# Linear attention beside a projection: decay exponents as differences of one kept sum, and low weight parts made by an adding DMA

## The reference, cut to what matters

```
cum   = cumsum(log_a)                                   # per channel k
att   = einsum('bthk,bshk,btshk->bhts', q, k, exp(cum_t - cum_s))   for s <= t
o     = att @ v + (q * exp(cum)) @ state
state = exp(cum_end) * state + (k * exp(cum_end - cum))^T @ v
```

## Time and profile before

| | |
|---|---|
| median of 3 runs | 1741.18 us (1737.77 to 1741.54) |
| the profiled execution's own time | 1737.67 us |
| its span | 1736.0 us |
| granted TensorE clock over the span | 0.988 |
| first projection in the span | about 44 to 295 us |

### The profile page before, as it was taken

One profiled execution on the slowest core, in us unless ns is written; L12 is line 12 of the kernel. 1 busy time (PEld: TensorE's weight loads), 2 busy tenths in 40 slices (PEclk: granted clock), 3 DMA queues, 4 the chain that ended last, 5 costly groups with the idle time before them and its releaser, 6 DMA issues. The chain is left out here.

```text
span 1736.0 us, 26342 instructions
## 1 busy us (share of the span) xinstructions
PE 1673.0 (96%) x10174; PEld 1416.8 (82%) x10174; DVE 1320.9 (76%) x2484; ACT 852.0 (49%) x1481; POOL 67.4 (4%) x120
## 2 busy tenths in 40 slices
PE   5899999799999999999999998999999999999998
PEld 1688877687888888878888657988898988999997
DVE  2777884786999999969984788599875555765586
ACT  3724345646555542256663665333354567665541
POOL 0940000000000000000000000000000000000000
PEclk7999999999999999999999999999999999999999
DMA  8543431042232236734554335444465554434443
GB/s 301 191 138 121 124 121 48 1 146 84 99 97 98 97 101 213 245 132 158 176 185 136 96 93 171 163 158 148 156 203 177 164 175 148 134 123 134 146 158 110
DMA packets 70325, 246.03 MB, mean 142 GB/s; under 512 B 8031, under 2 KB 9752, under 8 KB 69816
## 3 DMA queue, kind: packets, MB, share of 16 engines
q1 hardware_dynamic: 67736, 240.47, 42.3%
q10 hardware_dynamic: 2080, 2.76, 0.5%
q0 software_dynamic: 384, 1.11, 0.2%
HBM read 242.87 MB, written 1.18 MB: 141 GB/s over the span
## 5 line engine op out<-in xcount | busy, mean ns | idle before, releaser
L506 PE MATMUL banks<-m,weights_high 128*128 128x256 f32 (+1 forms) x4144 | 980.6, 330 | 10.0 <-DVE weights_low L373 7.2
L506 PEld LDWEIGHTS banks<-m,weights_high 128*128 128x128 f32 x4144 | 696.8, 190 | 90.1 <-issue 9.7
L506 PE MATMUL banks<-m,weights_low 128*128 128x256 f32 (+1 forms) x2072 | 676.9, 327 | 0.0
L373 DVE TENSOR_TENSOR weights_low<-weight_ring,weights_high 128x1024 fp32r<-128x1024 f32 x293 | 355.0, 1222 | 190.3 <-ACT weights_high L367 189.3
L506 PEld LDWEIGHTS banks<-m,weights_low 128*128 128x128 f32 x2072 | 392.7, 190 | 34.4
L367 ACT ACTIVATE weights_high<-weight_ring 128x1024 fp32r<-128x1024 f32 x293 | 309.1, 1057 | 223.3 <-DMA weight_ring<-in_weights 130.4
L675 DVE SCALAR_TENSOR_TENSOR m<-m,columns 128x189 f32<-128x189 f32 (+4 forms) x504 | 199.2, 470 | 11.5 <-ACT m L613 11.4
L831 DVE SCALAR_TENSOR_TENSOR m<-weight_ring,m 128x1024 bf16<-128x1024 f32 x160 | 195.8, 1224 | 8.2 <-ACT m L810 2.5
L506 PE MATMUL banks<-m,weight_ring 128*128 128x256 f32 x704 | 152.1, 379 | 0.0
L506 PEld LDWEIGHTS banks<-m,weight_ring 128*128 128x128 f32 x704 | 133.7, 190 | 18.1
L612 ACT ACTIVATE m<-banks,columns 128x512 f32<-128x512 f32 (+1 forms) x76 | 58.4, 768 | 170.4 <-PE banks L506 166.5
(11 more groups left out here) (423 smaller groups left out, 1720.6 us busy)
## 6 DMA issues: line engine op xcount, KB each, us to landing
weight_ring<-in_weights SPq DMA_DIRECT2D x433, 512.0 KB, 3.7
m<-entering SPq DMA_DIRECT2D x28, 256.0 KB, 3.2
x<-in_tokens SPq DMA_DIRECT2D x2, 1024.0 KB, 9.0
m<-in_cmp_w SPq DMA_DIRECT2D x1, 2048.0 KB, 7.4
m<-in_cond SPq DMA_DIRECT2D x2, 512.0 KB, 4.3
m<-entering POOLq DMA_DIRECT2D x4, 256.0 KB, 5.0
out<-x ACTq DMA_DIRECT2D x8, 128.0 KB, 2.0
m<-in_rg_w ACTq DMA_DIRECT2D x1, 512.0 KB, 3.5
```

The costliest lines, as they stand in the source:

```text
L373: dve.tensor_tensor(K.w_lo[:, g % PARTS, :], K.ring[:, PLACE[PRODUCT_BLOCKS[g]] % RING, :], K.w_hi[:, g % PARTS, :].bitcast(F32), ALU.subt ...
L506: mm = pe.matmul(out, lhsT, rhs, start=p.start and i == 0, stop=p.stop and i == len(passes) - 1)
```

## The change

It has two halves.

**Exponents.** The eighth `distances` moves to the front: PE makes the sums over each 128-token block once (`sums`, at the tick of level 1), ACT copies them out of PSUM into a kept tile `sums`, and the seven `distances` of the levels are gone. At level l DVE subtracts, from each element of the kept sum, that of its block's middle (two instructions of 128 x 1024), ACT takes the exponential in four pieces of 128 x 512 with the sign in `scale`, in place, and DVE multiplies as before. The scores of level l are made at the tick of level l+1 (one tick later), and DVE takes them up two ticks behind that, just ahead of the multiplications of level l+1. POOL makes only the masks of the levels (28 `affine_select` in place of 84), and the two strict masks later.

**Low parts.** For the projection's blocks from the ninth on (`BY_DMA`, blocks 8 to 30: 23 of them), DVE no longer subtracts. ACT writes the negated high part into `weights_low` (128 x 1024, behind a wait for its own high part), and POOL issues a DMA that adds the weight block from DRAM to it (`accum_op=ALU.add`, 512 KB each). PE waits for its landing, on one semaphore for each of the four buffers. The ring's place is released by the high part and not by the low part.

```diff
+EVEN_FIRST = 8
+BY_DMA = set(blocks_of("even_in")[EVEN_FIRST:])
@@ high_part
     act.activation(K.w_hi[:, g % PARTS, :], K.ring[:, place % RING, :], ACT.Copy).then_inc(*K.high_done.up())
+    if PRODUCT_BLOCKS[g] in BY_DMA:
+        act.wait_ge(*K.high_done.now())
+        act.activation(K.w_lo[:, g % PARTS, :], K.w_hi[:, g % PARTS, :].bitcast(F32), ACT.Copy,
+                       scale=-1.0).then_inc(*K.minus_done.up())
...
+def low_by_dma(K, pool, g, n):
+    pool.wait_ge(K.minus_done.sem, n)
+    pool.dma_start(K.w_lo[:, g % PARTS, :], K.dram["weights"][PLACE[PRODUCT_BLOCKS[g]]],
+                   accum_op=ALU.add).then_inc(K.low_landed[g % PARTS].sem, 16)
@@ _run_products
+        if PRODUCT_BLOCKS[g] in BY_DMA:
+            K.low_landed[g % PARTS].up(16)
+            K.parts_ready.append(K.low_landed[g % PARTS].now())
+            K.release[PLACE[PRODUCT_BLOCKS[g]]] = K.high_done.sem, g + 1
+            continue
...
-                    low_part(K, dve, n_low)
+                    if PRODUCT_BLOCKS[n_low] not in BY_DMA:
+                        low_part(K, dve, n_low)
...
+            for g, n in landing:
+                beside.half("gpsimd", pool, 2 * sum(d <= g for d in due))
+                low_by_dma(K, pool, g, n)
@@ GlaSteps.tensor_steps
         for l in range(1, GLEVELS + 1):
-            yield self.level(l)
-            pe.wait_ge(*self.taken.at(l))
-            pe.wait_ge(*self.tabled.at(l))
-            pe.wait_ge(*self.la_made.at(1))
-            distances(self.between[:, 2 * l - 2, :], self.between[:, 2 * l - 1, :])
-            yield self.level(l) + 3
+            if l == 1:
+                yield self.level(l)
+                pe.wait_ge(*self.taken.at(l))
+                pe.wait_ge(*self.la_made.at(1))
+                sums(K.tri_f[:], K.tri_b[:])
+            yield self.level(l + 1)
+            pe.wait_ge(*(self.taken.at(l) if l > 1 else self.sums_kept.at(1)))
             pe.wait_ge(*self.made.at(l))
             scores(self.factor[l % 2][:, 0, :, :], self.factor[l % 2][:, 1, :, :])
-        yield self.SUMS
-        pe.wait_ge(*self.taken.at(GLEVELS + 1))
-        distances(K.tri_f[:], K.tri_b[:])
@@ GlaSteps.scalar_steps
-            act.activation(e, self.banks(), ACT.Exp).then_inc(*self.exps.up())
+        act.activation(self.sums, self.banks(), ACT.Copy).then_inc(*self.sums_kept.up())
+        for l in range(1, GLEVELS + 1):
+            yield self.level(l) + 1
+            act.wait_ge(*self.differenced.at(l))
+            for d in range(2):
+                decay = e[:, 2 * d:2 * d + 2, :].rearrange("p a (b w) -> p (a b) w", w=size)
+                for part, sign in ((late, 1.0 - 2.0 * d), (early, 2.0 * d - 1.0)):
+                    ins = act.activation(decay[:, :, part], decay[:, :, part], ACT.Exp, scale=sign)
+            ins.then_inc(*self.exps.up())
@@ GlaSteps.vector_steps
+            yield self.level(l)
+            for d, middle in enumerate((half - 1, half)):
+                decay, total = (a[:, 2 * d:2 * d + 2, :].rearrange("p a (b w) -> p (a b) w", w=size) for a in (e, self.sums))
+                ins = dve.tensor_tensor(decay, total, total[:, :, middle:middle + 1].broadcast_to([P, 2 * T // size, size]),
+                                        ALU.subtract)
+            ins.then_inc(*self.differenced.up())
+            yield self.level(l) + 2
+            if l > 1:
+                take_scores(l - 1)
             dve.wait_ge(*self.exps.at(l))
```

More of the change, by code:

```diff
@@ L192, in __init__ @@
         self.low_done = count("weights_low_done")
+        self.minus_done = count("weights_high_negated")
+        self.low_landed = [count(f"weights_low_landed{i}") for i in range(PARTS)]
+        self.n_landing = 0
         self.used = count("weights_used")
@@ L1384, in feed_forward @@
                                 finish if half else None, Gate(gated_hi[:, j, :], gated_lo[:, j, :]) if half else None)
-                    rounds.append([Item(tile_products(first + (2 * j + half) * KD, KD,
-                                                      lambda k: h[:, k, :] if plain else K.h_parts(n, k), n), None, "act", conv)])
+                    tile = first + (2 * j + half) * KD
+                    whole = tile // TPB in PLAIN
+                    rounds.append([Item(tile_products(tile, KD, lambda k, whole=whole: h[:, k, :] if whole else K.h_parts(n, k), n),
+                                        None, "act", conv)])
             down = residual_items(K, f"down{layer}", KF, lambda k: (gated_hi[:, k, :], gated_lo[:, k, :]), t0,
@@ L1501, in __init__ @@
         self.la, self.att, self.cend = K.take(TT, 2 * 256), K.take(16, P), K.take(4, TT)
-        self.table = K.take(3 * GLEVELS + 2, P)
+        self.sums, self.table = K.take(4, T), K.take(GLEVELS, P)
         self.ss, self.rt = K.take(16), K.take(16)
-        self.between, self.masks, self.strict = (self.table[:, a:b, :] for a, b in ((0, 14), (14, 21), (21, 23)))
+        self.masks, self.strict = self.table, self.table[:, 0:2, :]
         self.e = f["gg"]
@@ L1510, in __init__ @@
         self.qc = mo.rearrange("p (i t) -> p i t", t=T)
[L1511 to L1513 removed]
+        sums = self.sums.rearrange("p i t -> p (i t)")
+        self.keys = sums.rearrange("p (c i) -> p c i", c=TT)
+        self.on = sums.rearrange("p (c v) -> p c v", v=GW)
         la = self.la.rearrange("p c i -> p (c i)")
@@ L1561, in pool_steps @@
             early, late = slice(0, half), slice(half, size)
-            fwd, bwd, mask, one = (a.rearrange("p (b w) -> p b w", w=size)
-                                   for a in (self.between[:, 2 * l - 2, :], self.between[:, 2 * l - 1, :],
-                                             self.masks[:, l - 1, :], ones))
+            mask, one = (a.rearrange("p (b w) -> p b w", w=size) for a in (self.masks[:, l - 1, :], ones))
             from_middle = (-half, 1, [[-size, n], [0, half]])
@@ L1569, in pool_steps @@
             for out, first, second in (
-                    (fwd[:, :, late], from_middle, (half, -1, [[size, n], [1, half]])),
-                    (fwd[:, :, early], (-1, 1, [[-size, n], [-1, half]]), to_middle),
-                    (bwd[:, :, early], (0, 1, [[-size, n], [-1, half]]), to_middle),
-                    (bwd[:, :, late], from_middle, (half - 1, -1, [[size, n], [1, half]])),
                     (mask[:, :, late], from_start, to_middle),
@@ L1578, in pool_steps @@
             ins.then_inc(*self.tabled.up())
+        yield self.level(4)
+        pool.wait_ge(*self.taken.at(3))
         pool.affine_select(out=self.strict[:, 0, :], in_=ones, compare_op=ALU.is_ge, fill=0.0, base=-1, pattern=[[-1, P]],
@@ L1709, in scalar_steps @@
         act.activation(e, e, ACT.Ln, bias=K.small[:, 1:2], scale=1.0).then_inc(*self.logged.up())
-        for l in range(1, GLEVELS + 2):
-            yield self.SUMS if l > GLEVELS else self.level(l)
-            act.wait_ge(*self.dists.at(l))
-            act.wait_ge(*(self.made.at(l - 1) if l > 1 else self.la_made.at(1)))
-            act.activation(e, self.banks(), ACT.Exp).then_inc(*self.exps.up())
+        yield self.level(1)
+        act.wait_ge(*self.dists.at(1))
+        act.activation(self.sums, self.banks(), ACT.Copy).then_inc(*self.sums_kept.up())
+        for l in range(1, GLEVELS + 1):
+            yield self.level(l) + 1
+            size, half = 1 << l, 1 << (l - 1)
+            early, late = slice(0, half), slice(half, size)
+            act.wait_ge(*self.differenced.at(l))
[4 more added lines that the diff above has]
+            ins.then_inc(*self.exps.up())
+        yield self.SUMS
+        act.wait_ge(*self.made.at(GLEVELS))
+        act.activation(e, self.sums, ACT.Exp).then_inc(*self.exps.up())
         yield self.KEYS[0]
@@ L1775, in vector_steps @@
         for l in range(1, GLEVELS + 1):
-            yield self.level(l) + 1
+            yield self.level(l)
             size, half = 1 << l, 1 << (l - 1)
             early, late = slice(0, half), slice(half, size)
+            if l == 1:
+                dve.wait_ge(*self.sums_kept.at(1))
+            else:
+                dve.wait_ge(*self.made.at(l - 1))
+            for d, middle in enumerate((half - 1, half)):
[6 more added lines that the diff above has]
+                take_scores(l - 1)
             dve.wait_ge(*self.exps.at(l))
@@ L1790, in vector_steps @@
             dve.tensor_tensor(k[:, :, late], bwd[:, :, late], gk[:, :, late], ALU.mult).then_inc(*self.made.up())
-            yield self.level(l) + 3
-            take_scores(l)
         yield self.SUMS + 1
+        take_scores(GLEVELS)
         dve.wait_ge(*self.exps.at(GLEVELS + 1))
```

16 lines of the change are left out of this document (9 added, 7 removed).

## The result

| | before | after |
|---|---|---|
| median | 1740.26 us (1737.77 to 1741.54, 4 runs) | 1713.97 us (1709.84 to 1717.71, 4 runs) |
| profiled execution, span | 1737.67, 1736.0 us | 1709.84, 1708.0 us |

What follows compares the result with a forecast made beforehand. PE's work was taken as the bound, with DVE becoming it in levels 4 to 7. -25.2 - 0.6 + 4.6 = -21.2 from the profiled 1737.67 gives 1716.5; the median lying 3.5 higher, 1720 us, range 1711 to 1742.

Steps and rivals of the forecast that it cites:

- PE's saving (-25.2): First projection on PE: eight exponent groups become one, seven times 3.6 us leave, level period 16.95 to 13.35 us.
- DVE becomes the bound in levels 4 to 7 (+4.6): Beside the convolutions DVE needs 14.5 us per level against PE's 13.35, so PE waits 1.15 us at four levels.
- a lead of DVE is not carried over: Levels 1 to 3 give DVE no lasting lead, since its convolution waits for PE's bank of the same item.
- The wait at the old eighth group (-0.6): A PE wait on DVE at the old eighth exponent group's place goes away; 0.6 us, an estimate.
- ACT (0): Negated copies of 1053 ns and split exponentials add 2.7 us per level on ACT, hidden in its idle time.
- the second rival: DVE and ACT wait for each other at the levels' exponentials, 2.4 us at each of seven: 1732 us; chance 0.17.
- The adding DMA (hidden): Between negated copy and block's first pass: lands in 7.4 us of at least 12.5 available, costing 3.1 us of the engines.
- The third rival: Adding DMA is the bound: PE waits on landings from block 8, binding from 4.2 us each; example 1782; chance 0.18.
- Sum: Whole kernel: -25.2 on PE, -0.6 for a wait, +4.6 for DVE make -21.2 us.
- the forecast's own case: Whole time at the forecast 1720 us, in its own range 1716 to 1725; chance 0.48.
- the first rival: The whole PE saving arrives, because DVE's 4.6 us in the levels don't appear: 1715 us; chance 0.12.

Runs made afterwards that it cites:

- the second comparison: The kernels before and after the change, both unedited, measured again on one chip: after 1715.95 us beside 1739.07 before, ratio 0.9863.
- the kernel with two more: Changed kernel plus two adding DMAs of 320 KB, into an unread tile, behind each of the 23; raw-row ring of 3 places: 1806.28 us, one run.

## Why the prediction was right, step by step

**PE's saving (-25.2).** Right. The period of a level without a wait is 13.38 us (forecast 13.35) where it was 16.95; seven times the difference is 25.0.

**DVE becomes the bound in levels 4 to 7 (+4.6).** The mechanism was right and is shown from both sides: the kernel with the exponents alone (period 16.8 with two more subtractions), the moved modulation blocks (the waits and the stretch shrink together by 2.4 and 2.6 us), and the products added on PE (the waits are used up first). The period was forecast at 14.5 and is 14.53. The term was a little too large, 3.8 in place of 4.6: level 4 waits 0.32 us and not 1.15. The step that was off is the sentence that a lead of DVE is not carried over. Its reason is right, since DVE loses most of the lead at the first tap, waiting for the bank; in the timeline of DVE after:

```profile
127.32 0.68 DVE L1838 TENSOR_TENSOR m<-m 128x512 f32<-128x512 f32 x1
...
134.10 2.73 DVE L700 SCALAR_TENSOR_TENSOR m<-m,columns 128x510 f32<-128x510 f32 x4 [3.70 <-ACT m L637]
```

The multiplications of level 3 end at 128.00, 4.69 us ahead of the scores at 132.69; where DVE is the bound, 0.15 us lie between the two. Of this lead of 4.54 us the wait takes 3.70, and the 0.84 left are what level 4 did not have to wait: 1.15 - 0.84 = 0.31.

**The wait at the old eighth group (-0.6).** PE did wait 0.61 us there in both profiles before, for DVE's masked copy, and no longer in the kernel with the low parts alone, which still has this group. (The 0.9 of the earlier trace rows is another wait, behind the keys.) S0 to the keys is 138.63 - 7 x 3.57 - 0.6 + 3.8 = 116.8, measured 116.73.

**ACT (0).** Right: its copies (1061 ns, forecast 1053) are hidden, and it is ACT that waits for DVE (17.9 us) and not the other way round, so the second rival fell.

**The adding DMA (hidden).** Right: PE never waits for one. Its engine price was forecast at 3.1 us and is 3.0. The Trainium skill (Collectives: The Full Stack, "Why ReduceScatter is half of AllGather") has an add at half a copy's rate, there for collectives. The trace agrees, with 2.05 times the engine time. Its landing was forecast at 7.4 us and took 5.6; beside the longer levels of the kernel with low parts alone it took 7.5. The share of the engines was given as 0.6 to 0.8 and was 0.84 to 0.89; the sum in the prediction itself, 12.2 of 14.5, gives 0.84, and in levels 1 to 3 the pair takes 13.4. The third rival was nearer than its chance tells: with 1.6 times the adding traffic the engines are full and PE waits.

**Sum.** -21.2 forecast, -22.1 measured in the stretch. The profile of the kernel after was forecast at 1716.5 us; its two profiled executions took 1709.84 and 1716.59. The forecast 1720 was 6 us above the first median and 4 above the second, and the first lies below the 1716 to 1725 given for the forecast's own case. Of the 6 us, 0.9 are the stretch, 0.9 the median before, which was taken as 1741.18 and came out at 1740.26 with a fourth run, and 4.2 lie outside the stretch, where the sum put nothing; in the second comparison 1.0 does. By the whole time alone the first rival, with its 1715, would have looked right. That would have been luck: the 3.8 us that it leaves out stand in the trace of each profile of this kernel.

**What stays open.** Why the rest of the program behind the stage takes 1436 us in one execution and 1443 in another, and why the clock of 20 to 40 us differs, was not followed further; nor what part of the 2.0 us by which the whole gains more than the stretch is the change's own. Of the adding DMA's capacity only one point above the forecast was measured, in one run; the kernel with two more was bound by a wait of GpSimd.

## What to carry to other kernels

When work leaves the engine that is the bound, sum the next engine's work over the new, shorter period before counting the gain: here each half of the change alone was worth 9.4 and 1.2 us, and both together 22.1. Relieve the second engine with one that shares nothing with it: ACT and the DMA engines took DVE's subtractions at no cost, while GpSimd, idle as it was, took 2.1 us from DVE for each 1.22. And compare a stretch between two marks of the trace beside the whole time when the effect is a few us: here the stretch repeated to 0.01 us where the rest of one kernel differed by 6.5. The stretch has to begin ahead of all that the change touches; this one begins behind GpSimd's tables, and may miss some 2 us for it.

## What the runs showed of the hardware

- An adding DMA of 512 KB from DRAM into the SBUF costs 3.0 us of the 16 engines, 2.05 times a plain load, lands in 5.6 us with the engines at 0.84 and in 7.8 with them full (7.5 in the kernel with the low parts alone, at 0.66 to 0.83); GpSimd is busy 0.87 us with its issue (20.0 us for 23, in the groups of the kernel after).
- A GpSimd subtraction of 128 x 1024 took 2.4 to 3.4 us, and a DVE operation of 0.68 us that met one of 2.7 us took 2.86.
- A DVE difference of 128 x 1024 with its second operand repeated over each block took 1218 ns, as a plain product of that shape did.
- The granted clock of levels 4 to 7 fell from 1.00 to 0.93 where PE had waits of 1.8 to 3.3 us in each level (the exponents alone), to 0.87 with the subtractions on GpSimd and to 0.80 with the late landings.
